# Feed-forward opening and block change written out tile by tile, x1's root mean square made in the attention stage, first group by token part

## The chip, the cores and the metric

The kernel runs on one core of one Trainium2 chip. The metric is the device time of one execution in microseconds, given as the median of three runs. A core has a matrix engine (PE, with its weight loads shown as PEld), a vector engine (DVE), a scalar engine (ACT), a general engine (POOL), and a sync engine (SP), whose queue issues most of the transfers. Each engine works through its own instructions in order and waits on semaphores that others raise.

## The reference, cut to what matters

One step of a streaming encoder layer: 2048 prompt frames (16 tiles of 128 rows) and 32 sample frames (tile 16, 32 rows), model width 1024. A token-mixing stage gives `x1 = x + rmsnorm(mix)`. Then comes the channel stage, with a hidden width of 4096:

```
u = rmsnorm(x1, norm_ffn_pre) @ w_up          # (tokens, 1024) @ (1024, 4096)
f = square(relu(u)) @ w_down                  # (tokens, 4096) @ (4096, 1024)
y = x1 + rmsnorm(f, norm_ffn_post)
rms_normalize(x) = x * rsqrt(mean(x * x) + eps)
```

## The kernel before, in words

Four stages follow one another, with a barrier between them: retention, projection of the attention inputs, `mix_phase` (attention, output projection, residual, x1 written to DRAM as `x1_scratch`) and `ffn_phase`. Only the last two are touched.

`mix_phase` works through 64 items (t, h): query tile t of 16, head h of 4. For each tile ACT squares and sums y (L1237, L1239), POOL raises the mean to the power -1/2 (L1154), DVE scales y (L1346), POOL adds the residual into `mix_xr` (L1161), and SP stores it (L1116), reloads `mix_xr` for the next tile (L1112) and then loads keys, queries and values of later tiles (L1095, L1098, L1101).

`ffn_phase` keeps all weights' use in 3-pass split form: each operand is a high part and a low part, and a product is three matmuls. Tokens are worked in two blocks: block 0 is tiles 0 to 7, block 1 is tiles 8 to 16. The hidden width is worked in 16 groups of 256 columns. In each block:

- The opening: for each tile x1 is loaded (L1629), ACT squares and sums it (L96, L99), POOL makes 1/rms (L108), DVE multiplies by it and the gain in place (L113), PE transposes it in 8 pieces into two PSUM banks (L120), ACT copies these out as the high part `ffn_hTh` (L130), and DVE subtracts to get the low part `ffn_hTl` (L136). Odd and even tiles use different pairs of the four banks `U`.
- For each group: `up` (PE, L1907) makes units of 24 matmuls into a bank of `U`. A unit is one half of the group's 256 columns for one part of the tokens (512 wide in block 0, 352 in block 1), so there are 4 units in block 0 and 6 in block 1. ACT takes the relu (L1744), DVE squares (L1823), ACT copies the high part (L1748), DVE subtracts for the low part (L1829). `down` (PE, L1923) makes two sums of 6 matmuls for each tile, and DVE adds them to the running sum `ffn_facc` (L1844; L1842 is the copy of the first group). The order on PE is up(g+1), then down(g).
- Weights of a group have one buffer: ACT copies the high part out of `ffn_raw` (L1717 up, L1723 down) and DVE makes the low part (L1793, L1800), once PE has read the last group's.

At the block change the last `down` of block 0 is interleaved with the opening of block 1, a tile of each in turn. ACT squares and sums the finished `ffn_facc` there (L1729, L1732), POOL makes 1/rms (L1681), and DVE normalises it in `hidden` of block 1's group 0 (L1806). POOL adds the residual (L1705), stores y (L1614) and loads the next residual tile (L1604). The `ffn_facc` of a tile is only written by block 1 once its store has landed.

## Time and profile before

| what | value |
|---|---|
| median of 3 runs | 3156.98 us (3156.43 to 3160.06) |
| the profiled execution's own time | 3157.81 us |
| its span | 3156.0 us |
| PE busy over the span | 92% |
| mix stage in the trace | about 930 to 1556.8 us |
| feed-forward stage in the trace | 1556.8 us to the end |

The profile gives for each instruction its start from the start of the span, its length, and in brackets the idle time of its engine just before it, with the instruction whose end released it. "issue" is a release that the profile doesn't show. The page has a row of PE's granted clock in tenths of full speed: 2.4 GHz is full, 1.2 GHz is half.

### The profile page before, as it was taken

The numbers are of one execution on the slowest core, as the hardware profiler recorded it, in microseconds if no ns is written. First come the engines' busy times: TensorE is split into PE (matmuls) and PEld (weight loads), VectorE is DVE, ScalarE is ACT, GpSimd is POOL, SyncE is SP. The second block draws the span as 40 slices with busy tenths as digits, with TensorE's granted clock in tenths as the row PEclk, the third lists the DMA queues.
The fourth block names the chain that finished last, engine by engine and source line by source line (L and its number), as shares of the span: only waits on it lengthen the run. The fifth ranks groups of instructions, "written<-read, shape, count | busy, mean of one in ns | idle before, by whom it ended". The sixth has DMA issues, their size and how long they took to land.

```text
span 3156.0 us, 39293 instructions
## 1 busy us (share of the span) xinstructions
PE 2898.0 (92%) x14977; PEld 2398.6 (76%) x14977; DVE 1515.4 (48%) x2983; ACT 926.9 (29%) x1838; POOL 318.4 (10%) x437
## 2 busy tenths in 40 slices
PE   5999995999968999999589999999968999999997
PEld 4888884778856766766468888888857998998995
DVE  3232333323246777777344444444456445445446
ACT  3222222222125555555331211211142211211212
POOL 0111110111112111111100000000013000000003
PEclk8999997999979999999789999999988999999999
DMA  4111003333332111110221111111124111111112
GB/s 147 32 34 34 34 21 116 111 113 123 117 122 75 64 64 47 52 41 21 107 68 46 54 40 53 40 53 53 40 69 136 51 40 41 53 40 40 53 54 97
DMA packets 105661, 204.64 MB, mean 65 GB/s; under 512 B 11024, under 2 KB 47888, under 8 KB 105552
## 3 DMA queue, kind: packets, MB, share of 16 engines
q1 hardware_dynamic: 103248, 194.79, 18.7%
q0 software_dynamic: 2304, 8.39, 0.8%
q8 instruction: 69, 1.13, 0.1%
q14 instruction: 40, 0.33, 0.0%
HBM read 168.28 MB, written 34.87 MB: 64 GB/s over the span
## 4 chain that ended last, share of the span: by engine, by line
PE 46%; DVE 2%; ACT 1%; DMA 1%; POOL 0%; issue 0%; SPq 0%; POOLq 0%
PE bank L1907 23%; PE bank L1923 22%; DVE ffn_facc L1806 1%; PE bank L120 1%; DVE ffnp_x L113 0%; ACT ffn_hTh L130 0%; DMA ffnp_x<-x_scratch 0%; DVE ffn_facc L1844 0%; POOL ffnp_rstd L108 0%; ACT ffn_relu L96 0%; ACT ffn_relu L1729 0%; DVE ffn_hidl L1829 0%; DMA ffn_raw<-in_w_up_dram 0%; DVE ffn_dnl L1800 0%; DVE ffn_upl L1793 0%
## 5 line engine op out<-in xcount | busy, mean ns | idle before, releaser
L1907 PE MATMUL bank<-ffn_hTh,ffn_uph 128*128 128x352 f32 (+1 forms) x1280 | 452.5, 354 | 23.3 <-DVE ffn_upl L1793 14.2
L1844 DVE TENSOR_TENSOR ffn_facc<-bank,ffn_facc 128x512 f32<-128x512 f32 x510 | 345.1, 689 | 233.4 <-PE bank L1923 233.0
L1907 PE MATMUL bank<-ffn_hTl,ffn_uph 128*128 128x352 f32 (+1 forms) x1280 | 451.5, 353 | 0.0
L1907 PE MATMUL bank<-ffn_hTh,ffn_upl 128*128 128x352 f32 (+1 forms) x1280 | 450.9, 352 | 0.0
L1923 PE MATMUL bank<-ffn_dnh,ffn_hidh 128*128 128x512 f32 x1088 | 427.3, 393 | 6.4 <-DVE ffn_dnl L1800 3.5
L1923 PE MATMUL bank<-ffn_dnh,ffn_hidl 128*128 128x512 f32 x1088 | 425.6, 391 | 0.0
L1923 PE MATMUL bank<-ffn_dnl,ffn_hidh 128*128 128x512 f32 x1088 | 425.5, 391 | 0.0
L1823 DVE SCALAR_TENSOR_TENSOR ffn_relu<-bank,ffn_relu 128x352 f32<-128x352 f32 (+1 forms) x160 | 94.5, 591 | 499.6 <-ACT ffn_relu L1744 499.6
L1907 PEld LDWEIGHTS bank<-ffn_hTh,ffn_uph 128*128 128x128 f32 x1280 | 242.6, 190 | 48.4 <-DVE ffn_upl L1793 14.5
L1907 PEld LDWEIGHTS bank<-ffn_hTl,ffn_uph 128*128 128x128 f32 x1280 | 242.7, 190 | 23.4
L1907 PEld LDWEIGHTS bank<-ffn_hTh,ffn_upl 128*128 128x128 f32 x1280 | 242.7, 190 | 22.7
L1744 ACT ACTIVATE ffn_relu<-bank 128x352 f32<-128x352 f32 (+1 forms) x160 | 83.0, 519 | 554.8 <-PE bank L1907 544.5
L1923 PEld LDWEIGHTS bank<-ffn_dnh,ffn_hidh 128*128 128x128 f32 x1088 | 205.8, 189 | 50.8 <-DVE ffn_facc L1844 4.6
L1723 ACT ACTIVATE ffn_dnh<-ffn_raw 128x1024 fp32r<-128x1024 f32 x64 | 64.5, 1052 | 607.8 <-PE bank L1923 590.5
L186 PE MATMUL bank<-retw_whi,retp_hTh 128*128 128x512 f32 x544 | 217.2, 399 | 26.1 <-DVE ret_rope_b L396 16.4
L1923 PEld LDWEIGHTS bank<-ffn_dnh,ffn_hidl 128*128 128x128 f32 x1088 | 205.4, 189 | 43.5
L1923 PEld LDWEIGHTS bank<-ffn_dnl,ffn_hidh 128*128 128x128 f32 x1088 | 205.5, 189 | 42.4
L1286 DVE TENSOR_SCALAR_CACHE_REDUCE mix_S<-bank 128x512 f32<-128x512 f32 (+4 forms) x320 | 175.3, 582 | 99.1 <-PE bank L1410 62.0
L186 PE MATMUL bank<-retw_wlo,retp_hTh 128*128 128x512 f32 x544 | 213.8, 393 | 0.0
L186 PE MATMUL bank<-retw_whi,retp_hTl 128*128 128x512 f32 x544 | 213.7, 393 | 0.0
L186 PE MATMUL bank<-dpw_whi,dpp_hTh 128*128 128x512 f32 x408 | 164.6, 403 | 8.9 <-DVE dpw_wlo L176 8.9
L1200 ACT ACTIVATE mix_S<-mix_S,mix_nm 128x128 f32<-128x128 f32 (+15 forms) x128 | 153.6, 1200 | 36.7 <-DVE mix_nm L1300 36.5
(196 smaller groups left out, 4462.3 us busy)
## 6 DMA issues: line engine op xcount, KB each, us to landing
ffn_raw<-in_w_up_dram SPq DMA_DIRECT2D x64, 512.0 KB, 4.4
ffn_raw<-in_w_down_dram SPq DMA_DIRECT2D x64, 512.0 KB, 4.1
ffnp_x<-x_scratch SPq DMA_DIRECT2D x24, 512.0 KB, 4.4
retp_x<-in_x_prompt_dram SPq DMA_DIRECT2D x16, 512.0 KB, 3.6
retw_raw<-in_w_in_dram SPq DMA_DIRECT2D x8, 1024.0 KB, 5.2
dpp_x<-in_x_prompt_dram SPq DMA_DIRECT2D x16, 512.0 KB, 5.1
dp_kst<-in_cache_diff_k_dram SPq DMA_DIRECT2D x32, 256.0 KB, 2.9
mix_xr<-in_x_prompt_dram SPq DMA_DIRECT2D x16, 512.0 KB, 3.3
```

Of the source, the lines that this page charges most:

```text
L120: last = self.nc.tensor.transpose(self.banks[2 * pair + k // 4][:, (k % 4) * P:(k % 4 + 1) * P], self.xn[u][:, k * P:(k + 1) * P], ident)
L186: last = self.nc.tensor.matmul(out, l[:, k, :], r[:, c, k, :], start=(k == 0 and q == 0), stop=(k == kt - 1 and q == 2))
L1200: nc.scalar.activation(S[n % 2][m][:, 0:width(t)], S[n % 2][m][:, 0:width(t)], ACT.Exp, bias=nm[n % 2][:, m:m + 1], accum_out=l[n % 2][:, ...
L1286: last = nc.vector.tensor_scalar(dst[:, c:c + whole], src[:, 0:whole], 1.0, None, ALU.mult, ALU.max, accum_out=mx[b][:, m, i + 1:i + 2])
L1723: nc.scalar.activation(dnh[:, i, :], raw[i][:], ACT.Copy).then_inc(s_whi, 1)
L1744: nc.scalar.activation(rh[i % 2][:, 0:w], U[i % s.ru][:, 0:w], ACT.Relu).then_inc(s_r, 1)
L1806: nc.vector.scalar_tensor_tensor(out=facc[:, i, :], in0=facc[:, i, :], scalar=rf[:, t:t + 1], in1=gain_b[:], op0=ALU.mult, op1=ALU.mult).t ...
L1823: nc.vector.scalar_tensor_tensor(out=rh[i % 2][:, 0:w], in0=U[i % s.ru][:, 0:w], scalar=0.0, in1=rh[i % 2][:, 0:w], op0=ALU.max, op1=ALU.m ...
L1844: nc.vector.tensor_tensor(out=part, in0=Dn[i % s.rd][:], in1=part, op=ALU.add).then_inc(s_add, 1)
L1907: last = nc.tensor.matmul(U[i % s.ru][:, 0:w], l[:, k, f * P:(f + 1) * P], r[:, k, c:c + w], start=(k == 0 and q == 0), stop=(k == 7 and q ...
L1923: last = nc.tensor.matmul(Dn[i % s.rd][:], l[:, f, tile * P:(tile + 1) * P], r[:, f, n * N:(n + 1) * N], start=(f == 0 and q == 0), stop=( ...
```

## The change

It has five parts.

1. x1's mean square is made in `mix_phase`: ACT `meansq_x` at head 3 of each tile and POOL `rstd_x`, kept in a column of `keep.rstd_x` for each tile. SP's reload of `mix_xr` now waits for the square as well.
2. `ffn_phase` has no mean square, so the chain for a tile is load, DVE `norm_x`, PE `x_transpose`, ACT `x_hi`, DVE `x_lo`. All tiles use one pair of banks, `U[2:4]`, and each half tile has its own wait.
3. The first group takes its units by token part (`first_units`), in banks `U[0]` and `U[1]`. The order on PE, ACT and DVE is written out by hand: in block 0 the first unit starts after tile 3.
4. Tiles 8 to 11 are loaded during block 0, and normalised by DVE in its last but one step. The block change is written out by hand as well, and the last two tiles of the last `down` come after the first group's units.
5. ACT's `meansq_f` and DVE's `norm_f` of block 0's result move from the opening and group 0 of block 1 to group 1, and the residual loads on POOL's queue wait for tiles 10 and 11 to be transposed.

```diff
@@ mix_phase, SP and ACT
                 def residual_rows(j):
+                    if j:
+                        sp.wait_ge(s_sx, j)
                     sp.dma_start(xr[0:rows(j), :], xv[j - 1] if j else x_s[0]).then_inc(s_x, 16)
...
+                def meansq_x(j):
+                    m = rows(j)
+                    act.wait_ge(s_x1, j + 1)
+                    nc.scalar.activation(junk[0:m, :], xr[0:m, :], ACT.Square, accum_out=sx[0:m, :]).then_inc(s_sx, 1)
+                    act.wait_ge(s_sx, j + 1)
+                    if j:
+                        act.wait_ge(s_rx, j)
+                    nc.scalar.activation(mean_x[0:m, :], sx[0:m, :], ACT.Copy, scale=1.0 / 1024,
+                                         bias=NORM_EPS).then_inc(s_mx, 1)
...
                     if h == 3:
+                        if t:
+                            meansq_x(t - 1)
                         y_out(t, 0)
@@ ffn_phase
         U, Dn = banks[0:4], banks[4:8]
+        TT = U[2:4]
...
+                self.first_units = [(f, c, w) for c, w in self.subs for f in range(FG)]
...
-            if t >= 2:
-                if b and i - 2 >= by_dve:
-                    eng.wait_ge(s_yd, i - 1 - by_dve)
-                else:
-                    eng.wait_ge(s_y, t - 1 if i >= 2 else blocks[b][0])
+            if b == 0 and i < 2:
+                eng.wait_ge(s_xT, 2 * (10 + i) + 2)
+            elif b and i - 2 >= by_dve:
+                eng.wait_ge(s_yd, i - 1 - by_dve)
+            else:
+                eng.wait_ge(s_y, t - 1 if i >= 2 else b1[0])
@@ ffn_phase, DVE
-                                for n in range(2 * i - 2, min(2 * i, ended.nb)):
+                                for n in range(max(2 * i - 4, 0), min(2 * i - 2, ended.nb)):
                                     norm_f(ended, n)
...
                         if not last:
-                            hidden(s, g + 1, 1 - e)
+                            hidden(s, g + 1, 1 - e, shapes[0] if s.b and isinstance(g, int) and g == 0 else None)
...
                                 accumulate(s, g, tile)
+                                if s.b == 0 and near and 1 <= tile <= 4:
+                                    norm_x(7 + tile)
@@ ffn_phase, PE
+                def x_transpose(t):
+                    pe.wait_ge(s_xn, t + 1)
+                    for b in range(2):
+                        if t:
+                            pe.wait_ge(s_lo, 2 * t - 1 + b)
+                        for k in range(4):
+                            last = nc.tensor.transpose(TT[b][:, k * P:k * P + rows(t)],
+                                                       x[slots[t]][0:rows(t), (4 * b + k) * P:(4 * b + k + 1) * P],
+                                                       ident[0:rows(t), 0:rows(t)])
+                        last.then_inc(s_xT, 1)
...
+                    if s.b == 0:
+                        for t in range(4):
+                            x_transpose(t)
+                        first_up(s, 0, range(0, 4))
+                        x_transpose(4)
+                        first_up(s, 0, range(4, 8))
+                        x_transpose(5)
+                        first_up(s, 1, range(0, 4))
+                        x_transpose(6)
+                        first_up(s, 1, range(4, 8))
+                        x_transpose(7)
+                        first_up(s, 2)
+                        first_up(s, 3)
+                        pe.wait_ge(s_pad, 4)
+                    else:
                         pe.wait_ge(s_h, s.u0)
...
+                        x_transpose(8)
+                        down(shapes[0], G - 1, 1, 0)
+                        x_transpose(9)
+                        down(shapes[0], G - 1, 1, 1)
+                        x_transpose(10)
+                        down(shapes[0], G - 1, 1, 2)
+                        first_up(s, 0, range(0, 4))
+                        x_transpose(11)
+                        first_up(s, 0, range(4, 8))
+                        x_transpose(12)
+                        first_up(s, 1)
+                        x_transpose(13)
+                        down(shapes[0], G - 1, 1, 3)
+                        first_up(s, 2)
+                        x_transpose(14)
+                        first_up(s, 3)
+                        x_transpose(15)
+                        down(shapes[0], G - 1, 1, 4)
+                        x_transpose(16)
+                        down(shapes[0], G - 1, 1, 5)
+                        first_up(s, 4)
+                        first_up(s, 5)
+                        down(shapes[0], G - 1, 1, 6)
+                        down(shapes[0], G - 1, 1, 7)
```

On PE at block 0's opening the order before is all eight tiles' transposes (here the last two tiles) and then the first unit:

```order
L120 MATMUL bank0<-kept_ident,ffnp_x2 128x128 x4
L120 MATMUL bank1<-kept_ident,ffnp_x2 128x128 x4
L120 MATMUL bank2<-kept_ident,ffnp_x3 128x128 x4
L120 MATMUL bank3<-kept_ident,ffnp_x3 128x128 x4
L1907 MATMUL bank0<-ffn_hTh,ffn_uph 128x512
```

In the changed kernel the same place on PE reads as follows, from tile 2 (`ffn_x2`) on:

```order
L2043 MATMUL bank2<-kept_ident,ffn_x2 128x128 x4
L2043 MATMUL bank3<-kept_ident,ffn_x2 128x128 x4
L2043 MATMUL bank2<-kept_ident,ffn_x3 128x128 x4
L2043 MATMUL bank3<-kept_ident,ffn_x3 128x128 x4
L2052 MATMUL bank0<-ffn_hTh,ffn_uph 128x512
```

The first unit moved from behind tile 7 to behind tile 3, and all transposes are in banks 2 and 3.

On DVE at the block change the order before is the up weights' low parts, then for each tile the norm, the two sums and the two low parts:

```order
L1793 TENSOR_TENSOR ffn_upl<-ffn_raw1,ffn_uph 128x1024
L113 SCALAR_TENSOR_TENSOR ffnp_x0<-ffnp_x0,ffnp_rstd0,ffnp_gain 128x1024
L113 SCALAR_TENSOR_TENSOR ffnp_x1<-ffnp_x1,ffnp_rstd1,ffnp_gain 128x1024
L1844 TENSOR_TENSOR ffn_facc<-bank4,ffn_facc 128x512
L1844 TENSOR_TENSOR ffn_facc<-bank5,ffn_facc 128x512
```

In the changed kernel, on DVE:

```order
L1865 TENSOR_TENSOR ffn_upl<-ffn_raw1,ffn_uph 128x1024
L1884 TENSOR_TENSOR ffn_hTl<-bank2,ffn_hTh 128x4x128
L1884 TENSOR_TENSOR ffn_hTl<-bank3,ffn_hTh 128x4x128
L1933 TENSOR_TENSOR ffn_facc<-bank4,ffn_facc 128x512
L1933 TENSOR_TENSOR ffn_facc<-bank5,ffn_facc 128x512
L1884 TENSOR_TENSOR ffn_hTl<-bank2,ffn_hTh 128x4x128
L1884 TENSOR_TENSOR ffn_hTl<-bank3,ffn_hTh 128x4x128
```

The norms have gone from the front of the block change, and the low parts of tile 8 stand straight behind the weights' low parts.

On DVE in group 1 of block 1 (352 wide; `ffn_gain_f` is the gain after the feed-forward) the changed kernel has the norms of block 0's result:

```order
L1911 TENSOR_TENSOR ffn_hidl1<-ffn_relu1,ffn_hidh1 128x352
L1891 SCALAR_TENSOR_TENSOR ffn_facc<-ffn_facc,ffn_rstd_f,ffn_gain_f 128x1024 x2
L1905 SCALAR_TENSOR_TENSOR ffn_relu1<-bank0,ffn_relu1 128x352
L1911 TENSOR_TENSOR ffn_hidl1<-ffn_relu0,ffn_hidh1 128x352
L1891 SCALAR_TENSOR_TENSOR ffn_facc<-ffn_facc,ffn_rstd_f,ffn_gain_f 128x1024 x2
```

Before, the same norms stood in group 0, on DVE:

```order
L1829 TENSOR_TENSOR ffn_hidl0<-ffn_relu0,ffn_hidh0 128x352
L1806 SCALAR_TENSOR_TENSOR ffn_facc<-ffn_facc,ffn_rstd_f,ffn_gain2 128x1024 x2
L1823 SCALAR_TENSOR_TENSOR ffn_relu0<-bank2,ffn_relu0 128x352
L1829 TENSOR_TENSOR ffn_hidl0<-ffn_relu1,ffn_hidh0 128x352
L1806 SCALAR_TENSOR_TENSOR ffn_facc<-ffn_facc,ffn_rstd_f,ffn_gain2 128x1024 x2
```

They moved one group later, with the same two norms behind a unit.

## Rows read from the trace of the kernel before

**Rows 1.** The page's busy times over the whole span.

```profile
PE 2898.0 (92%) x14977; PEld 2398.6 (76%) x14977; DVE 1515.4 (48%) x2983; ACT 926.9 (29%) x1838; POOL 318.4 (10%) x437
```

**Rows 2.** Waits of PE from 1550 us to the end: total, times, longest.

```profile
PE bank L120 <- DVE ffnp_x L113: 57.5, 15, 19.5
PE bank L1907 <- DVE ffn_upl L1793: 14.2, 1, 14.2
```

**Rows 3.** Chain of waits, 1540 to 2450 us: start, length, what.

```profile
1594.04 24.24 PE bank L1907 x96
1618.28 5.46 issue
...
2391.15 25.68 PE bank L1907 x144
2416.83 24.51 PE bank L1923 x108
```

**Rows 4.** Timeline of the opening of block 0.

```profile
1561.29 0.22 DVE L1852 MEMSET ffn_hidh<- 128x192 f32 x1 [10.76 <-DMA ffnp_gain<-in_norm_ffn_pre_dram]
...
1577.64 1.94 PE L120 MATMUL bank<-kept_ident,ffnp_x 128*128 128x128 f32 x8 [3.25 <-DVE ffnp_x L113]
1578.61 1.28 DVE L113 SCALAR_TENSOR_TENSOR ffnp_x<-ffnp_x,ffnp_rstd,ffnp_gain 128x1024 f32<-128x1024 f32 x1
1579.62 1.09 ACT L130 ACTIVATE ffn_hTh<-bank 128x512 fp32r<-128x512 f32 x2 [2.84 <-PE bank L120]
...
1592.69 1.29 DVE L136 TENSOR_TENSOR ffn_hTl<-bank,ffn_hTh 128x512 fp32r<-128x512 f32 x2 [1.15 <-ACT ffn_hTh L130]
```

**Rows 5.** Timeline of the block change, PE, DVE, ACT.

```profile
2286.87 0.39 PE L1923 MATMUL bank<-ffn_dnh,ffn_hidl 128*128 128x512 f32 x1
2288.38 2.36 DVE L1800 TENSOR_TENSOR ffn_dnl<-ffn_raw,ffn_dnh 128x1024 fp32r<-128x1024 f32 x2 [0.40 <-ACT ffn_dnh L1723]
2295.70 1.06 ACT L1717 ACTIVATE ffn_uph<-ffn_raw 128x1024 fp32r<-128x1024 f32 x1 [1.00 <-DMA ffn_raw<-in_w_up_dram]
2296.78 1.23 DVE L1793 TENSOR_TENSOR ffn_upl<-ffn_raw,ffn_uph 128x1024 fp32r<-128x1024 f32 x1 [0.83 <-ACT ffn_uph L1717]
2300.13 1.94 PE L120 MATMUL bank<-kept_ident,ffnp_x 128*128 128x128 f32 x8 [12.88 <-DVE ffnp_x L113]
...
2311.88 1.06 PE L120 MATMUL bank<-kept_ident,ffnp_x 128*128 128x128 f32 x8 [2.31 <-DVE ffnp_x L113]
```

**Rows 6.** Timeline of ACT: two units 352 wide at full clock.

```profile
2365.54 0.47 ACT L1744 ACTIVATE ffn_relu<-bank 128x352 f32<-128x352 f32 x1 [2.99 <-PE bank L1907]
2369.38 0.47 ACT L1744 ACTIVATE ffn_relu<-bank 128x352 f32<-128x352 f32 x1 [2.99 <-PE bank L1907]
```

**Rows 7.** Timeline of DVE and POOL, group 0 of block 1.

```profile
2363.07 2.48 DVE L1806 SCALAR_TENSOR_TENSOR ffn_facc<-ffn_facc,ffn_rstd_f,ffn_gain 128x1024 f32<-128x1024 f32 x2
2368.11 4.66 DVE L1806 SCALAR_TENSOR_TENSOR ffn_facc<-ffn_facc,ffn_rstd_f,ffn_gain 128x1024 f32<-128x1024 f32 x2
2369.26 2.42 POOL L1705 TENSOR_TENSOR ffn_facc<-ffn_facc,ffnp_x 128x1024 f32<-128x1024 f32 x1
2373.68 3.42 POOL L1705 TENSOR_TENSOR ffn_facc<-ffn_facc,ffnp_x 128x1024 f32<-128x1024 f32 x1 [0.59 <-DMA ffnp_x<-x_scratch]
2378.10 0.51 DVE L1823 SCALAR_TENSOR_TENSOR ffn_relu<-bank,ffn_relu 128x352 f32<-128x352 f32 x1
2378.54 2.72 DVE L1829 TENSOR_TENSOR ffn_hidl<-ffn_relu,ffn_hidh 128x352 fp32r<-128x352 f32 x1
```

**Rows 8.** Timeline of ACT and SP in the mix stage, tiles 2 and 9.

```profile
991.73 0.60 ACT L1232 ACTIVATE mix_y<-bank 128x512 f32<-128x512 f32 x1 [1.12 <-PE bank L1438]
...
993.98 0.60 ACT L1211 ACTIVATE mix_AT<-bank 128x512 f32<-128x512 f32 x1 [0.95 <-PE bank L1451]
...
1246.28 1.06 ACT L1237 ACTIVATE mix_junk<-mix_y 128x1024 bf16<-128x1024 f32 x1
...
1221.39 0.33 SPq L1112 DMA_DIRECT2D mix_xr<-in_x_prompt_dram  x1
1237.63 0.33 SPq L1098 DMA_DIRECT2D mix_qn<-q_scratch  x1
```

More of the change, by code:

```diff
@@ L1155, in rstd_y, with rstd_x @@
                                             op=ALU.pow).then_inc(s_ry, 1)
+                def rstd_x(j):
+                    m, t = rows(j), j - 1 if j else nt
+                    pool.wait_ge(s_mx, j + 1)
+                    nc.gpsimd.tensor_tensor(out=keep.rstd_x[0:m, t:t + 1], in0=mean_x[0:m, :], in1=half[0:m, :],
+                                            op=ALU.pow).then_inc(s_rx, 1)
                 def residual(j):
@@ L1733, in meansq_f, with relu @@
                                          bias=NORM_EPS).then_inc(s_mf, 1)
-                def hidden(s, g, e):
+                def relu(s, g, i, units):
+                    f, c, w = units[i]
                     k0 = s.u0 + g * s.ku
+                    bank = U[i % 2] if units is s.first_units else U[i % s.ru]
+                    act.wait_ge(s_u, k0 + i + 1)
+                    if i >= 2:
+                        act.wait_ge(s_hl, k0 + i - 1)
+                    nc.scalar.activation(rh[i % 2][:, 0:w], bank[:, 0:w], ACT.Relu).then_inc(s_r, 1)
@@ L1751, in _ @@
+                            if ended is not None:
+                                for n in range(2 * i - 2, min(2 * i, ended.nb)):
+                                    meansq_f(ended, n)
                 for s in shapes:
                     w0 = 2 * G * s.b
-                    if s.b:
-                        act.wait_ge(s_u, s.u0)
-                        act.wait_ge(s_hl, s.u0)
-                        up_hi(w0 + 1, s)
-                    pre.act_meansq(act, slot(s.t0), loads(s.t0), s.t0 + 1)
@@ L1758, in _ @@
-                    for i, t in enumerate(s.tiles):
-                        if i + 1 < s.nb:
-                            pre.act_meansq(act, slot(t + 1), loads(t + 1), t + 2)
-                        pre.act_hi(act, t, t + 1, rows(t), i % 2)
-                        if s.b == 0 and i == 1:
-                            up_hi(1, s)
-                        if s.b and i:
-                            meansq_f(shapes[0], i - 1)
-                    hidden(s, 0, 0)
+                    fu = s.first_units
@@ new lines, in up_unit, with first_up @@
+                def up_unit(bank, unit, ks):
+                    f, c, w = unit
+                    for k in ks:
+                        for q, (l, r) in enumerate(parts(uph, upl, hTh, hTl)):
+                            last = nc.tensor.matmul(bank[:, 0:w], l[:, k, f * P:(f + 1) * P], r[:, k, c:c + w],
+                                                    start=(k == 0 and q == 0), stop=(k == 7 and q == 2))
+                    return last
+                def first_up(s, i, ks=range(8)):
+                    f, c, w = s.first_units[i]
+                    if i == 0 and ks[0] == 0:
+                        pe.wait_ge(s_wlo, 4 * G * s.b + 2)
+                    if f == 0 and ks[0] == 0:
+                        pe.wait_ge(s_lo, 2 * (s.t0 + (c + w - 1) // P) + 2)
+                    if i >= 2 and ks[0] == 0:
+                        pe.wait_ge(s_h, s.u0 + i - 1)
+                    last = up_unit(U[i % 2], s.first_units[i], ks)
+                    if ks[-1] == 7:
+                        last.then_inc(s_u, 1)
@@ L1898, in up @@
                 def up(s, g):
-                    first = isinstance(g, int) and g == 0
-                    pe.wait_ge(s_wlo, 4 * G * s.b + (2 if first else 4 * g))
+                    second = isinstance(g, int) and g == 1
+                    pe.wait_ge(s_wlo, 4 * G * s.b + 4 * g)
                     k0 = s.u0 + g * s.ku
-                    for i, (f, c, w) in enumerate(s.units):
-                        if not (first and s.b == 0 and i < s.ru):
-                            pe.wait_ge(s_h, k0 + i + 1 - s.ru)
-                        for k in range(8):
-                            for q, (l, r) in enumerate(parts(uph, upl, hTh, hTl)):
-                                last = nc.tensor.matmul(U[i % s.ru][:, 0:w], l[:, k, f * P:(f + 1) * P],
-                                                        r[:, k, c:c + w], start=(k == 0 and q == 0),
-                                                        stop=(k == 7 and q == 2))
-                        last.then_inc(s_u, 1)
+                    for i, unit in enumerate(s.units):
+                        pe.wait_ge(s_h, k0 if second and i < s.ru else k0 + i + 1 - s.ru)
+                        up_unit(U[i % s.ru], unit, range(8)).then_inc(s_u, 1)
```

352 lines of the change are left out of this document (231 added, 121 removed).

## The prediction

> **What bounds the kernel now.** The page's busy times come first: PE is busy 92% of the span, DVE 48% [rows 1], so time is won only where PE stands idle. The waits of PE behind 1550 us say where that is in the feed-forward stage: 57.5 us in 15 waits of the transposes for x1's norm and 14.2 us in one wait for the up weights' low part [rows 2]. The chain of waits dates them. The first unit starts at 1594.04, group 0's four units end at 1618.28, and 5.46 us follow until up(1) [rows 3]. At the block change PE ends block 0's last but one `down` at 2287.26 (2286.87 + 0.39) and stands 12.88 us before the first transpose [rows 5]; each further tile waits about 2.3 us for its norm, as in the row at 2311.88 [rows 5]; up(1) of block 1 only starts at 2391.15 [rows 3]. The 14.2 us lie just ahead of that. The sum is made against the profiled execution's own time, 3157.81 us, of which 3156.0 is span; it is 0.83 us above the median 3156.98.
>
> **Opening of block 0.** The mean square and the 1/rms leave the tile's chain. DVE then waits for the gain's transfer, which landed at about 1561.3 when it was first in the queue [rows 4]. It is now second, behind x tile 0; with about 0.4 us for one more issue, the first norm starts at 1561.7. Ahead of the first unit DVE has five norms of 1.25 (1.28 with its start [rows 4]), four pairs of low parts of 1.25 (1.29 for two [rows 4]) and two weights' low parts, which I price at 2.3 (2.36 for two of that size [rows 5]): 5.0 + 6.25 + 2.3 = 13.6. About 0.65 is lost until the first tile is transposed and copied and 0.3 at tile 3, so the first unit starts at 1561.7 + 13.6 + 0.95 = 1576.3, 17.8 us earlier. From there the four units took 24.24 us [rows 3], their slow start included. Into them come four tiles' transposes. At full clock the eight cost 1.06, at half clock 1.94 [rows 4, 5]; I take 1.1, as PE is in steady work by then: 4.4 us. Unit 2 needs tile 7's low parts, queued on DVE behind `square` and norms: 1.5 us. The group ends at 1576.3 + 24.2 + 4.4 + 1.5 = 1606.4, which is 11.9 us earlier. The 5.46 us behind it stay, since the up weights' low part still needs the end of the last unit and no `down` lies there. **Gain 12.** Bounds: 6, if the transposes run at half clock (+3.5) and each tile waits half a microsecond more for its banks; 15, if the loads and transposes hide entirely.
>
> **Block change.** Tiles 8 to 11 are normalised by then. Their norms (1.28 each) stand on DVE in a `down` of block 0 whose sums leave it idle half the time, so they cost nothing there. If that cover failed they would cost 4 x 1.28 = 5. From 2287.26 the first transpose goes at once. `down` then waits for its weights until 2290.74 [rows 5]: 2.4 us. After tile 0's two sums (2.7) PE waits for tile 8's low parts, since these stand on DVE behind the up weights' low parts, which end at 2298.0 [rows 5]; with 0.65 for the first low part tile 9's transpose starts at 2298.7: 5.2 us idle. That is the first wait left, and what is late is the weight's transfer. After it I find none over 1 us: PE always has a half unit or a `down` while ACT and DVE finish the tile. PE's own work to up(1) is 8 full transposes of 1.06, one of a quarter's width (8.7 in all), 16 sums of 1.36 (24.51 / 18 [rows 3]) = 21.8, and six units of 3.84 (from relu to relu [rows 6]) = 23.0: 53.5. With 2.4 + 5.2 idle, 0.8 for tile 16's norm and 3 us for half clock after the two pauses, 64.9: up(1) starts at T = 2352.2. The up weights' low part for it is ready by about T - 1, made during the last four sums, so the 14.2 us vanish. This is 39 us ahead of 2391.15.
>
> **What group 1 gives back.** up(1) takes 23.0 instead of 25.68 [rows 3] (+2.7), so it ends 41.6 us earlier. Then `down` needs DVE, which now has the eight norms of the finished result behind the units. With the first at T + 13 (unit 1's end, two squared sums on ACT, relu of unit 2), DVE has 8 x 1.25 for norms, and 8 x 0.44 for squares and low parts: 13.5, to T + 26.5. But POOL's residual adds run at the same time. A pair of norms takes 2.48 us alone and 4.66 with an add of 2.42 in it; a low part, both of whose inputs are in SBUF, takes 2.72 where others take some 0.5; a square, with an input in a PSUM bank, keeps its 0.51 [rows 7]. So an add takes about 2.1 from DVE, and six fall in: 12.6, and DVE reaches the first sum at T + 39. PE ends up(1) at T + 23 and has three banks to fill, to T + 27: 12 us idle. Behind the first two sums stand the next up weights' low parts (2.3, and an add's 2.3); three banks cover some of it, and I take 2 more. **Net of the block change and group 1:** 41.6 - 14 = 27.6, say 27. Bounds: 41 if the adds cost nothing, 18 if all eight cost 2.42 and the pauses keep PE at half clock twice as long.
>
> The Trainium skill, page "SBUF — State Buffer", section "Who interferes with whom", says that a VectorE instruction with two SBUF inputs and a GpSimd one that reads SBUF exclude each other for a whole instruction. By it eight adds of 2.42 would be 19.4 us if none fell into DVE's own idle time, and the sums out of PSUM would stay free. The rows agree: the low part waits, the square doesn't.
>
> **Mix stage.** ACT gains per tile a square as at L1237 (1.06) and a read of the sum and a scale (0.2 each), about 1.4, 17 times: 24. It stands just ahead of `y_out` of head 3. At tile 2 ACT stands 1.12 us before that instruction and 0.95 before the copy after the next exp [rows 8], 2.07 together, and this is the least of the 15 tiles from 1 on. So it costs 0; without that cover it would cost 24. POOL's 17 powers of 0.55 lie in its waits. SP reloads `mix_xr` at 1221.39 and then stands until 1237.63 for PE [rows 8]; the reload moves by some 4 us and nothing behind it moves. At the stage's end the last mean square runs beside the store of x1 and its landing: I take 0, at most 0.5.
>
> **Sum.** 3157.8 - 12 - 27 = 3118.8; against the median 3118.
>
> **Rivals.**
> - *The adds are cheap.* If POOL's adds fall into DVE's own waits, `down` starts at once: 12 more, 3106. For it: ACT paces group 1 too (two squared sums, a relu and a copy per unit of 3.84), so DVE has idle time. Against it: 4.66 against 2.48.
> - *One pair of banks.* Before, tiles alternate between two pairs; now a tile's transposes wait for the last one's low parts. If a tile is then serial (1.94 + 1.09 + 1.29 = 4.3 [rows 4] against DVE's 2.5), the four tiles ahead of the first unit cost 7 more and the later ones 4, and in group 1 the stores of y are late as well: 3126 to 3132. Against it: each half has its own wait, so PE fills one bank while the other is emptied. The Trainium skill, page "Perfetto Trace Analysis", section "Matmuls", advises rotating independent groups through different banks so that the emptying overlaps; this change gives up half of the rotation, and by that rule its opening would be worth 5 and not 12.
> - *Nothing won.* The deferred norms, adds and stores take back all: `down` of group 0 waits for stores of y that land later than T + 60. It takes adds 7 us apart and a wait of 39. Against it: two adds are 4.4 apart (2369.26 and 2373.68 [rows 7]), and `down` of group 0 reaches the last tile only at about T + 59.
> - *Slower: the mix stage's reload on the path.* SP's reload of `mix_xr` waits for ACT's square, 4.2 us later, and the key and query loads stand behind it. If each of 16 tiles became 4.2 us longer, that is 67 against a gain of 39: 3186. It decides from 2.4 us per tile. Against it: SP stands 16 us behind the reload for PE anyway [rows 8].
>
> **How the numbers follow.** Chances: forecast 0.62 (3110 to 3126), adds cheap 0.12, banks or stores dearer 0.20, nothing won 0.03, slower 0.03. A difference of 0.2% (6 us) is about what can be told from none. Faster therefore 0.94, same 0.03, slower 0.03. The range goes from the cheap adds, 3104, to 3132 (dearer banks).
>
> **What would show it.** The first unit should start near 1576 and up(1) of block 0 near 1612; the block change should show waits of 2.4 and 5 us and up(1) near 2340 (2352 less the opening's 12); `down` of group 0 in block 1 should wait some 12 us for DVE, with norms of 4.7 a pair beside adds. In the mix stage ACT should be busier by 24 us with the end at 1557. It is wrong if that stage ends later than 1560, if the first unit waits for loads, or if `down` doesn't wait.

## The result

The changed kernel took 3139.36 us (median of 4 runs, 3133.6 to 3139.44), beside 3158.52 for the kernel before on the same chip: a ratio of 0.9928 over all runs, 95% interval 0.9914 to 0.9941 (the two medians alone give 0.9939). The forecast was 3118, with a range up to 3132, so the time lies 7 us outside the range. The sign was right; of the gain of 39 us that was forecast, 19 came. The profiled execution took 3139.41 us, with a span of 3137.6. All reading below is made against it.

### The profile after

The busy times of the whole span, as in [rows 1]:

```profile
PE 2911.7 (93%) x14977; PEld 2397.1 (76%) x14977; DVE 1516.0 (48%) x2983; ACT 925.8 (30%) x1838; POOL 315.0 (10%) x437
```

The span is 18.4 us shorter, and yet PE is busy 13.7 us *more*, with the same 14977 matmuls. Waits went away and matmuls became longer. That is the first sign of something that the forecast had no term for.

The waits of PE from 1550 us on, which answer to [rows 2] (total, times, longest):

```profile
PE bank L2043 <- DVE ffn_x L1878: 17.9, 2, 17.5
PE bank L2088 <- DVE ffn_facc L1931: 15.2, 1, 15.2
PE bank L2043 <- DVE ffn_hTl L1884: 7.2, 4, 2.9
PE bank L2088 <- DVE ffn_dnl L1872: 6.2, 2, 3.5
PE bank L2052 <- DVE ffn_upl L1865: 5.5, 1, 5.5
PE bank L2052 <- DVE ffn_hTl L1884: 3.2, 2, 1.7
```

Of the 57.5 us 17.9 are left, nearly all of them the one wait at the stage's start, and the 14.2 us at the block change are gone; the 5.5 us in the fifth line are the 5.46 us of "issue" that [rows 3] has behind group 0 of block 0. The new line is the second: in group 1 of block 1 `down` stood 15.2 us until VectorE came to its sums.

The chain of waits, pieces that answer to [rows 3, 5] (start, length, what):

```profile
1558.93 5.39 DMA ffn_gain_x<-in_norm_ffn_pre_dram
...
1579.26 5.46 PE bank L2052 x12
...
1615.54 14.57 PE bank L2052 x54
1639.86 22.25 PE bank L2088 x96
1662.11 22.26 PE bank L2052 x96
...
2289.07 5.36 DMA ffn_raw<-in_w_up_dram
...
2297.52 1.16 PE bank L2043 x8
2298.68 4.36 PE bank L2088 x12
...
2349.26 11.49 PE bank L2052 x72
2391.52 23.97 PE bank L2088 x90
2415.49 22.91 PE bank L2052 x144
...
2726.04 25.02 PE bank L2088 x108
```

Two groups of block 0 in the kernel before, from the same view, for the comparison:

```profile
1648.42 21.81 PE bank L1923 x96
1670.23 22.26 PE bank L1907 x96
```

A `down` of 96 matmuls takes 22.25 us where it took 21.81; one of 108 takes 25.02 where it took 24.51 [rows 3]. The `up` beside it kept its 22.26. TensorE's granted clock is full in both. The difference is small, but block 0 has 16 groups and block 1 as many.

The span is made up of stretches whose ends both chains date. With them the gap of 20.6 us (forecast 3118.8 for the profiled execution, measured 3139.4) can be laid out. Positive is time lost against the forecast:

| stretch | forecast | measured | gap |
|---|---|---|---|
| end of the attention stage | 1556.9, unchanged | 1558.6 | +1.7 |
| opening, to `up`(1) of block 0 | 12 won | 9.9 won | +2.1 |
| groups 1 to 15 of block 0 | nothing | 15 downs of +0.44 | +6.6 |
| block change, to `up`(1) of block 1 | 39 won | 40.2 won | -1.2 |
| group 1 of block 1, to `up`(2) | 12 given back | 16 given back | +4 |
| the rest of block 1 | nothing | 14 downs of +0.51, and the end | +7.4 |

These add up to the 20.6. "12 given back" is the block change's 39 less the net 27 of the forecast; the 16 are 66.2 us from 2349.26 to 2415.49, less the 50.2 from 2391.15 to 2441.34 in the kernel before. Of the 4 us of that row 0.5 is again the longer `down`; most of the rest is TensorE's wait, 15.2 us where 12 was forecast.

### The profile page after: what moved, and what is told of

Its sections match the earlier page's. It is cut to its first block, busy times and chain, and to the rows that moved or that the text cites. A ratio compares the mean times of both kernels' runs of the same rounds, so it can differ in the third digit from the quotient of the medians.

```text
span 3137.6 us, 39331 instructions
## 1 busy us (share of the span) xinstructions
PE 2911.7 (93%) x14977; PEld 2397.1 (76%) x14977; DVE 1516.0 (48%) x2983; ACT 925.8 (30%) x1838; POOL 315.0 (10%) x437
## 4 chain that ended last, share of the span: by engine, by line
PE 47%; DVE 2%; POOL 1%; DMA 0%; ACT 0%; issue 0%; SPq 0%; POOLq 0%; DVEq 0%
PE bank L2088 24%; PE bank L2052 23%; DVE ffn_facc L1891 1%; PE bank L2043 0%; POOL ffn_facc L1738 0%; DVE ffn_facc L1933 0%; DVE ffn_upl L1865 0%; DVE ffn_hTl L1884 0%; DMA ffn_gain_x<-in_norm_ffn_pre_dram 0%; DMA ffn_raw<-in_w_up_dram 0%; DVE ffn_dnl L1872 0%; POOL ffn_rstd_f L1720 0%; DVE ffn_x L1878 0%; DMA ffn_x<-x_scratch 0%; DVE ffn_facc L1898 0%
## 5 line engine op out<-in xcount | busy, mean ns | idle before, releaser
L2088 PE MATMUL bank<-ffn_dnh,ffn_hidh 128*128 128x512 f32 x1088 | 431.8, 397 | 24.2 <-DVE ffn_facc L1931 15.2
L2088 PE MATMUL bank<-ffn_dnh,ffn_hidl 128*128 128x512 f32 x1088 | 432.6, 398 | 0.0
```

The costliest lines, as they stand in the source:

```text
L2088: last = nc.tensor.matmul(Dn[i % s.rd][:], l[:, c:c + P], r[:, f, n * N:(n + 1) * N], start=(f == 0 and q == 0), stop=(f == FG - 1 and q = ...
```

## Experiments

### Why `down` became longer

The new code changed two things that `down` reads. The hidden buffers are flat, with rows of 1056 columns instead of 1152 and in another order, and all large buffers begin 32 bytes above a multiple of 64, where they began at one.

**Address.** The changed kernel with 32 bytes put in:

```diff
+        sb("shift", [P, 8])
         hTh, hTl = sb("hTh", [P, 8, tokens], F32R), sb("hTl", [P, 8, tokens], F32R)
```

> The changed kernel with 32 unused bytes per partition ahead of the transposed activations, so that every large buffer of the feed-forward stage begins at a multiple of 64 bytes, as in the kernel before, instead of 32 above one; nothing else differs. Theory 1 (the addresses make the down matmuls dear): a down of 108 matmuls takes 24.51 us again instead of 25.02, one of 96 takes 21.81 instead of 22.25, so about 14 us come back and the time is near 3125. Rival (the flat layout of the hidden buffers does it): both stay at 25.02 and 22.25, and the time stays at 3139.

Measured: 3140.55 us, ratio 0.995 (0.9934 to 0.9967); the downs stay at 22.25 and 25.02. The mirror image is the kernel before with the same line.

> The kernel before with 32 unused bytes per partition ahead of the transposed activations, so that its large buffers lie 32 bytes above multiples of 64. By the theory of addresses its downs grow from 24.51 to 25.02 us and from 21.81 to 22.25, and the time by 14 us to about 3172; by the theory of the layout nothing changes, 3158.

Measured: 3163.03 us, ratio 1.0014 (1.0004 to 1.0023), which is some 4 us where the theory of addresses wanted 14. Its downs stay at 21.81 and 24.51, and the span of its profiled execution is 3155.3, 0.7 less than before. By these rows the theory of addresses fell; what made its other executions longer (up to 3167.1 us) no trace shows.

**Layout.** The old buffers in the new kernel:

```diff
-        hidden_flat = [[sb(f"hid{n}{u}", [P, FG * tokens + P - dec], F32R) for n in "hl"] for u in range(2)]
+        hid3 = [[sb(f"hid{n}{u}", [P, FG, nb_max * P], F32R) for u in range(2)] for n in "hl"]
```

> The changed kernel with the hidden activations in the four buffers of the kernel before (2 x 1152 columns each, high parts of both generations first, then low parts), all still 32 bytes above a multiple of 64; the square's scratch output lies in the gain's buffer, to make room. If the layout makes the down matmuls dear, their rows go back to 24.51 and 21.81 us and the time to about 3125; if it is the addresses modulo 64, the rows stay at 25.02 and 22.25 and the time at 3139.

Measured: 3127.35 us, ratio 0.9907 (0.9891 to 0.9924). Its chain of waits:

```profile
1643.73 21.81 PE bank L2088 x96
...
2719.30 24.51 PE bank L2088 x108
```

The layout it is: the median is 12 us under that of the changed kernel and 13 under that of a_shift32, which ran on the same chip. In the traces the feed-forward stage alone is 16.0 us shorter (3126.6 less its start at 1563.57, against 3137.6 less 1558.56). Of these, 14 are the downs of groups 1 to 15, as in the table above; the others lie in the opening, the block change and group 1. Two more runs part its two halves, the order of the four buffers and the pitch of their rows.

> The changed kernel with its flat hidden buffers (rows of 1056 columns) allotted in the order of the kernel before: high 0, high 1, low 0, low 1. If the distance between the high and the low part (8832 bytes in the changed kernel, 18432 before, 17664 here) makes the down matmuls dear, a down of 108 goes back to 24.51 us and one of 96 to 21.81. If the 1056-column rows do it, they stay at 25.02 and 22.25.

> The changed kernel with hidden rows of 1152 columns, as before, but in the changed kernel's order: high 0, low 0, high 1, low 1 (9216 bytes from high to low); the square's scratch output lies in the gain's buffer. If the row pitch is what counts, down takes 24.51 and 21.81 us; if the order is, 25.02 and 22.25.

Measured: the order alone, 3142.6 us in one run, with downs of 22.26 and 25.04; the pitch alone, 3128.0 us, with 21.81 and 24.51. It is the pitch. Which pitches are good was then tried with one for each parity of the group:

```diff
+        pitch = (1088, 1184)
+        hidden_flat = [[sb(f"hid{n}{u}", [P, max(2 * pitch[u], pitch[u] + nb_max * P)], F32R) for n in "hl"] for u in range(2)]
...
-                            c = f * tokens + tile * P
+                            c = f * pitch[e] + tile * P
```

> The changed kernel with hidden rows of 1088 columns in the buffers of even groups and 1184 in those of odd ones (4352 and 4736 bytes; 1056 is 4224, 1152 is 4608). If any pitch above 1056 will do, both kinds of down take 24.51 us. If the pitch must be a whole number of 512 byte rows, so that all 128-column slices keep their offset within 512 bytes, both stay at 25.02. If a multiple of 256 bytes is enough, the even ones take 24.51 and the odd ones 25.02.

Measured: 3135.65 us. The chain of waits, groups 0 and 1 of block 0 and two neighbours of block 1:

```profile
1643.56 21.81 PE bank L2090 x96
...
1687.63 22.25 PE bank L2090 x96
...
2724.44 25.04 PE bank L2090 x108
...
2772.39 24.51 PE bank L2090 x108
```

Neighbouring groups differ by just the 0.44 and 0.5 us. A larger pitch isn't better as such: 1088 columns (4352 bytes) are good and 1184 (4736) are not. Of the four pitches, 1088 and 1152 are multiples of 256 bytes, 1056 and 1184 are not. With 1184 every slice of the second hidden row begins 128 bytes off those of the first, modulo 256. Yet it isn't only the second row's matmuls that are long: in the odd groups of block 0 the six matmuls of a sum come 231.2 ns apart on average in the first row and 232.3 in the second, where the even groups have 227.4 and 227.0.

**The other operand.** `up` had 231.9 ns for each 512-column matmul in both kernels. Its moving operand is `hTh`/`hTl`, and that has rows of 1056 columns too.

> The changed kernel with rows of 1152 columns in the transposed activations instead of 1056; the hidden rows stay at 1056. To make room, the output norm multiplies by the first gain, and the second isn't loaded. The up matmuls 512 wide take 231.9 ns each before and after the change, the slow figure of down. If the pitch of the moving operand does that, an up of 96 takes 21.81 us instead of 22.26 in block 0; if only the stationary operand's pitch counts, up stays at 22.26. Down stays at 22.25 and 25.02 in either case.

Measured: 3136.84 us. The chain of waits in block 0:

```profile
1642.93 22.25 PE bank L2085 x96
1665.18 21.77 PE bank L2049 x96
```

(This kernel makes room by using one gain for both norms.) Now `up` is the shorter one, 21.77 us, and `down` keeps its 22.25. The old kernel had paid this all along in block 0.

### What group 1 gave back

The DVE and POOL timelines of the changed kernel in group 1 (T, the start of `up`(1), is 2349.26):

```profile
2362.14 2.47 DVE L1891 SCALAR_TENSOR_TENSOR ffn_facc<-ffn_facc,ffn_rstd_f,ffn_gain_f 128x1024 f32<-128x1024 f32 x2
...
2368.32 0.57 POOL L1720 TENSOR_TENSOR ffn_rstd_f<-ffn_meansq_f,ffn_half 128x1 f32<-128x1 f32 x1
2368.86 2.40 POOL L1738 TENSOR_TENSOR ffn_facc<-ffn_facc,ffn_x 128x1024 f32<-128x1024 f32 x1
2368.93 3.42 DVE L1891 SCALAR_TENSOR_TENSOR ffn_facc<-ffn_facc,ffn_rstd_f,ffn_gain_f 128x1024 f32<-128x1024 f32 x1 [0.48 <-POOL ffn_rstd_f L1720]
2371.55 0.60 POOL L1650 DMA_DIRECT2D out_dram<-ffn_facc  x1 [0.30 <-POOL ffn_facc L1738]
2372.15 0.54 POOL L1640 DMA_DIRECT2D ffn_x<-x_scratch  x1
...
2390.79 1.27 DVE L1931 COPY ffn_facc<-bank 128x512 f32<-128x512 f32 x2
```

Two norms alone take 2.47 us; five single ones take 3.36 to 3.42 each. Each of the five begins when POOL's 1/rms ends, and just then POOL begins its next add. POOL makes the 1/rms of tile t + 2 between the load behind add t - 1 and add t, so norm and add start together every time. VectorE reaches the first sum (line L1931) at T + 41.5; the forecast said T + 39.

**All 1/rms ahead of the adds.**

```diff
-                    for t in s.tiles[:2]:
+                    lead = s.tiles if s.b == 0 else s.tiles[:2]
+                    for t in lead:
                         rstd_f(t)
                     for i, t in enumerate(s.tiles):
-                        if i + 2 < s.nb:
+                        if s.b and i + 2 < s.nb:
                             rstd_f(t + 2)
```

> The changed kernel with all eight powers of block 0's output norm ahead of GpSimd's first residual add, instead of each two tiles ahead. If group 1 loses its 15.2 us because each norm waits for a power that stands behind an add in GpSimd's queue, the norms end with ScalarE's last mean square (T + 23) plus one or two adds' contention, VectorE ends hidden(1) about 9 us earlier, at T + 32, TensorE's wait falls from 15.2 to 6 us, and the time to about 3130. If it is the adds' contention itself, wherever the powers stand, the norms stay near 3.4 us each and the wait stays over 12 us, the time at 3137 to 3139.

Measured: 3134.1 us, ratio 0.9927 (0.9911 to 0.9944). DVE's timeline:

```profile
2384.23 1.27 DVE L1932 COPY ffn_facc<-bank 128x512 f32<-128x512 f32 x2
...
2397.42 1.29 DVE L1932 COPY ffn_facc<-bank 128x512 f32<-128x512 f32 x2 [4.62 <-DMA out_dram<-ffn_facc]
```

VectorE came to the sums at T + 31, as the first theory said, but TensorE's waits only fell from 15.2 to 10.2 us, in six pieces. Behind them is something that neither theory had: a sum of block 1 overwrites the rows of `facc` that a store of block 0 still reads. The adds now began so late that their stores were the next in line. So the adds must start early, and the 1/rms must not stand behind them.

**Four, two, two.** On the kernel with the old hidden buffers:

```diff
+                    ahead = iter(s.tiles)
                     for i, t in enumerate(s.tiles):
-                        if i + 2 < s.nb:
-                            rstd_f(t + 2)
+                        for _ in range((3 if i == 0 else 1) if s.b else (4, 2, 2)[i] if i < 3 else 0):
+                            n = next(ahead, None)
+                            if n is not None:
+                                rstd_f(n)
```

> The kernel of run b_hid_3d (3127) with GpSimd's powers of block 0 in the order four, add 0, two, add 1, two, add 2, and the rest of the adds. With all eight ahead VectorE reached the first sum 6 us earlier, at T + 35, but the adds and stores ended so late that the sums of down(0) stood for stores. Worked out here: norms 0 to 3 lie ahead of the adds, 4 to 7 beside adds 1 and 2, VectorE reaches the first sum at T + 34 and the last store lands at T + 49, about when tile 7's sum comes. TensorE then loses some 8 us in place of 15.2, and the time is 3120 to 3121. Rival: stores bound it, as with all powers ahead, and the waits sum up to over 12 us: 3125 to 3127.

Measured: 3119.6 us, ratio 0.9866 (0.9849 to 0.9882), 8 us under run b_hid_3d. In the traces 6.6 of them lie in group 1: `up`(1) to `up`(2) took 65.7 us there and takes 59.0 here. TensorE's wait is one of 8.9 us, and VectorE reaches the sums at T + 35.

**Without the adds.** What the rest is made of:

```diff
-                        nc.gpsimd.tensor_tensor(out=facc[0:rows(t), i, :], in0=facc[0:rows(t), i, :],
-                                                in1=xe[i % 2][0:rows(t), :], op=ALU.add).then_inc(s_y, 1)
+                        if s.b:
+                            nc.gpsimd.tensor_tensor(out=facc[0:rows(t), i, :], in0=facc[0:rows(t), i, :],
+                                                    in1=xe[i % 2][0:rows(t), :], op=ALU.add).then_inc(s_y, 1)
+                        else:
+                            pool.sem_inc(s_y, 1)
```

> The kernel of run f_powers_4_2_2 without GpSimd's eight residual adds of block 0 (that block's output is then without its residual); stores and loads stay. If the adds take from VectorE what stays of group 1's wait (8.9 us), each pair of norms takes 2.5 us, VectorE reaches the first sum at T + 28 and TensorE waits under 3 us, so the time is 3113 to 3115. If the eight norms and the 2 x 6 squares and low parts are simply too much for the group, the wait stays over 6 us.

Measured: 3110.68 us in one run, some of it an early end of the attention stage. The 8.9 us shrink to three waits:

```profile
PE bank L2092 <- DVE ffn_facc L1935: 1.6, 3, 0.9
```

All four pairs of norms take 2.47 or 2.48 us, and VectorE reaches the sums at T + 27.2. So 7.3 of the 8.9 us were the adds, and VectorE's own load hides behind TensorE's `up`(1) and first banks but for 1.6 us. The Trainium skill, page "SBUF — State Buffer", section "Who interferes with whom", has a VectorE instruction with two SBUF inputs and a GpSimd one that reads SBUF exclude each other for a whole instruction; by that rule the pair of norms should drop to its time alone once no add runs, and the trace agrees.

### Why the attention stage ended later

It ended at 1556.86 us before and at 1558.56 after. In all but one of the other kernels with the changed attention stage it ended later still, mostly near 1562, with TensorE's waits in the stage as they were (47.8 us in 23 waits for `mix_S` before, 47.0 in 23 after). Windows of PE at the change from tile 8 to tile 9, first in the kernel before, then in the changed one (PE busy, count, granted clock as a share of full speed, DMA share, GB/s):

```profile
1216.00:1218.00 2.00, 1.24 (x6) 1.00 0.00 0
1218.00:1220.00 2.00, 0.38 (x4) 1.00 0.24 98
1220.00:1222.00 2.00, 1.97 (x13) 1.00 0.41 164
1222.00:1224.00 2.00, 2.00 (x12) 1.00 0.77 253
```

```profile
1216.00:1218.00 2.00, 1.01 (x6) 1.00 0.01 4
1218.00:1220.00 2.00, 0.59 (x4) 1.00 0.36 150
1220.00:1222.00 2.00, 1.97 (x8) 0.53 0.28 113
1222.00:1224.00 2.00, 2.00 (x7) 0.62 0.00 0
```

TensorE paused 2.4 us in both (4 us less 1.62 and less 1.60 busy). Before, it went on at full clock; after, about 3.4 us ran at the lower of its two levels. That costs (1 - 0.53) x 2 + (1 - 0.62) x 2 = 1.7 us, which is this tile's share. (The stage itself is 2.7 us longer in this trace, 634.1 us from its gain's load at 924.43 where it was 631.5 from 925.41; the stages ahead of it happened to end 1.0 us earlier.)

The changed attention stage alone, in front of the old feed-forward stage:

> The kernel before with the changed attention stage alone: x1's mean squares and powers are made there as in the changed kernel, but nothing reads them, and the feed-forward stage is the old one. If the 24 us of ScalarE work are covered, as predicted, the feed-forward stage starts at 1556 to 1557. If the work moves PE's pauses into stretches of half clock, it starts at 1559 to 1564 and the whole is 2 to 7 us longer than before, 3160 to 3165.

Measured: 3167.87 us, the feed-forward stage starting at 1562.93: 6 us later. The squares behind the output copy in ACT's order, on the kernel of run f_powers_4_2_2:

```diff
+                        y_out(t, 0)
                         if t:
                             meansq_x(t - 1)
-                        y_out(t, 0)
```

> The kernel of run f_powers_4_2_2 (3119.6) with x1's mean square of a tile behind the first output copy of the next in ScalarE's order instead of ahead of it. Its attention stage ended at 1563 like most with the mean squares. If the squares' place ahead of the output copy costs these 6 us, the stage ends at 1557 and the time is 3114. If it is only a matter of which pauses of TensorE the clock answers with a stretch at half speed, TensorE's waits stay the same 47 us and the end lies anywhere from 1557 to 1564.

Measured: 3124.76 us, start at 1564.78. The place isn't it. Another trace of the kernel before, unchanged:

> The kernel before, unchanged, for another trace of its attention stage. In two traces with the old stage the feed-forward stage starts at 1556.9 and 1556.1 us, in eleven with the mean squares at 1558.6 to 1564.8. If the mean squares cost the difference, it starts at 1556 to 1557 again; if the spread is the chip's, anywhere up to 1564.

Measured: 3157.08 us, start at 1556.62. And the squares and powers left out, on the fastest kernel (below):

```diff
+                nc.gpsimd.memset(keep.rstd_x[:], 1.0)
...
-                    if j:
-                        sp.wait_ge(s_sx, j)
...
-                        if t:
-                            meansq_x(t - 1)
```

> The kernel of run v_pitch_per_block without x1's mean squares and powers in the attention stage; the root mean square is taken as 1, so the feed-forward stage computes with x1 unnormalised in scale, and SyncE's reload waits for no square. Three traces of the old attention stage ended 5 us earlier than the mean of thirteen with the squares (1556.5 against 1561.9). If the squares cost that, the feed-forward stage starts at 1556 to 1557 and all ends 5 us earlier than with them. If it is the lottery of which pause the clock answers, it starts anywhere between 1556 and 1565.

Measured: 3107.86 us, start at 1557.13, and no drop of the clock at that tile change:

```profile
1220.00:1222.00 2.00, 1.97 (x13) 1.00 0.53 217
1222.00:1224.00 2.00, 2.00 (x11) 1.00 0.65 211
```

Four traces have no squares there (before, c_before_shift32, q_before_again, w_no_squares). They start the feed-forward stage at 1556.1 to 1557.1, mean 1556.7. Fourteen traces with the squares ahead of the output copy start it at 1558.1 to 1565.6, mean 1561.9. In these profiled executions the squares go with 5 us, though TensorE waits no longer for anything.

The times of the other executions don't bear this out as a cost in general. The traced executions of the kernel before took 3157.1 and 3157.8 us, but its 40 others on record average 3160.3 (3155.0 to 3166.1). The seven kernels with the squares that ran more than once go the other way: their 22 other executions average 2.0 us less than the traced ones. If the feed-forward stage takes as long in each execution as in its kernel's trace, the attention stage ends at about 1559.6 on average without the squares and 1559.8 with them. This is an estimate, since no trace dates the stage in those executions, but by it the traces of the kernel before were early ones, and a cost of the squares is not shown. The one run of k_mix_alone speaks for a cost (it lies above all seven runs of the kernel before on its chip, 3158.3 to 3164.0), and it can't decide.

Which of TensorE's pauses are followed by the lower clock also differs between kernels whose attention stage is the same code; why, these runs don't show.

### The opening

The first norm waited 5.39 us for the gain, which was second in SP's queue. The gain first, on the kernel of the next section:

```diff
+                        sp.dma_start(gain_x[:], gain_pre.to_broadcast([P, 1024])).then_inc(s_gain, 16)
                         x_tile(0)
-                        sp.dma_start(gain_x[:], gain_pre.to_broadcast([P, 1024])).then_inc(s_gain, 16)
```

> The kernel of run n_pitch_1088 with the gain's transfer ahead of tile 0's in SyncE's queue. The first norm waited for the gain, 5.4 us behind its issue. If the second transfer in the queue always lands last, the norm waits for tile 0 instead and starts as late, 5.8 us after the stage's start; if the gain itself is the slow one, it starts 0.4 us earlier. The time is that of n_pitch_1088 within 1 us apart from where the attention stage ends.

Measured: the first norm starts 5.76 us after the stage, against 5.74 with the gain second, and waits for tile 0's transfer, 5.29 us. Whichever is second lands last. (The run took 3122.79 us, with a start of the stage at 1565.58.)

### Faster kernels

First one pitch for all, 1088 columns:

```diff
+        pitch = -(-tokens // 64) * 64
...
-        hTh, hTl = sb("hTh", [P, 8, tokens], F32R), sb("hTl", [P, 8, tokens], F32R)
+        hTh, hTl = sb("hTh", [P, 8, pitch], F32R), sb("hTl", [P, 8, pitch], F32R)
...
+        hid_flat = [[sb(f"hid{n}{u}", [P, pitch + nb_max * P], F32R) for n in "hl"] for u in range(2)]
```

> The kernel of run f_powers_4_2_2 (3119.6) with rows of 1088 columns (4352 bytes, a multiple of 256) in both the transposed activations and the hidden buffers; the three small statistics share one buffer to make room. If a row pitch that is a multiple of 256 bytes makes each 512-column matmul 5 ns shorter whichever operand it feeds, up of 96 takes 21.8 us in block 0 instead of 22.26 and down stays at 21.81 and 24.51: 16 x 0.48 = 7.7 us, near 3112. Rival: the moving operand needs another multiple (1152 columns are 9 times 512 bytes), up stays at 22.26 and the time at 3119.

Measured: 3114.59 us, ratio 0.9853 (0.9836 to 0.987). The chain of waits:

```profile
1638.69 21.76 PE bank L2092 x96
1660.45 21.76 PE bank L2056 x96
...
2701.66 24.50 PE bank L2092 x108
2726.16 23.23 PE bank L2056 x144
```

Block 0's `up` fell to 21.76 us as expected. Block 1's, whose units are 352 wide, rose from 22.92 to 23.23, and 15 x 0.31 = 4.7 us of the 16 x 0.5 = 8 go back. So block 0 alone got another pitch, as a second view of the same buffers:

```diff
-        hTh, hTl = sb("hTh", [P, 8, tokens], F32R), sb("hTl", [P, 8, tokens], F32R)
+        hT = sb("hTh", [P, 8 * tokens], F32R), sb("hTl", [P, 8 * tokens], F32R)
+        views = [[a[:, 0:8 * n].rearrange("p (k n) -> p k n", k=8) for a in hT] for n in (len(b0) * P, tokens)]
```

> The kernel of run f_powers_4_2_2 (3119.6) with block 0's transposed activations in rows of 1024 columns (4096 bytes), a second view of the same buffers; block 1 keeps its 1056, since in run n_pitch_1088 rows of 1088 made its 352 wide up of 144 longer, 23.23 us instead of 22.92, while block 0's up of 96 fell to 21.76. If a multiple of 256 bytes is the rule for the 512 wide matmul, up takes 21.8 us in block 0 and 22.92 in block 1: 16 x 0.5 = 8 us less than 3119.6, near 3112. Rival: rows of exactly 4096 bytes are dear again for both operands and up stays at 22.26, 3119.

Measured: 3112.02 us, ratio 0.9841 (0.9828 to 0.9855), the lowest median with the full computation. The interval overlaps that of n_pitch_1088, but the traces tell them apart: from its start to the end of the span the feed-forward stage takes 1548.3 us here and 1553.7 there. Its chain:

```profile
1643.09 21.76 PE bank L2090 x96
1664.85 21.76 PE bank L2054 x96
...
2703.57 24.51 PE bank L2090 x108
2728.08 22.92 PE bank L2054 x144
```

## Why the prediction was right in sign and wrong in size

- **What bounds the kernel.** Right: the gain lay in TensorE's waits around the opening and the block change. 9.9 and 40.2 us came of them, 50 in all; what the total lacks was lost in other places.
- **Block change, 39 us.** Right: 40.2. The two waits foreseen at 2.4 and 5.2 us measured 2.67 and 2.93:

```profile
2289.10 0.80 PE L2088 MATMUL bank<-ffn_dnh,ffn_hidh 128*128 128x512 f32 x1 [2.67 <-DVE ffn_dnl L1872]
2297.52 1.16 PE L2043 MATMUL bank<-kept_ident,ffn_x 128*128 128x128 f32 x8 [2.93 <-DVE ffn_hTl L1884]
```

The second is shorter than foreseen because the 12 matmuls between the two ran at half clock and took 5.5 us (2289.10 to 2294.59) where 2.8 is usual; the 12 behind it took 4.36. Waits and half clock together are 9.9 us against the forecast's 10.6 (2.4 + 5.2 + 3). The cause named for them is right too: the weights' transfer (2289.07, 5.36 us) is in the chain.

- **Opening, 12 us.** Mis-sized: 9.9. The gain landed 5.39 us behind its issue and the first norm started 5.8 us after the stage's start, where 4.8 was counted; the units and transposes took 30.8 us instead of 30.1. The bound of 6 to 15 held it.
- **"Groups 1 to 15 cost the same".** This step was never written down, and it is the one that failed: the sum took each unchanged group at its old price. The new hidden buffers have rows of 1056 columns, and each `down` matmul takes 231.7 ns instead of 227. That is 15 x 0.44 = 6.6 us in block 0 and 14 x 0.51 = 7.1 in block 1, two thirds of the gap. Runs h_pitch_1152 and g_flat_order settle it. With the old pitch (run b_hid_3d) the kernel measured 3127.35 us, inside the forecast's range, so this one term put at nothing decides that the time missed it.
- **What group 1 gives back.** The mechanism was right: adds take VectorE's time from the norms, the wait is for `facc`, and without adds it is 1.6 us. The size was off: 15.2 for that wait against 12, and 16 given back against 12 (0.5 of it the longer `down`). The step "six adds fall in, 2.1 each" left out that the 1/rms stands behind an add in POOL's queue, which adds 0.5 to 1.0 us of waiting per norm and starts each of the last five norms together with an add.
- **Rival: adds cheap.** Refuted by the same rows. **Rival: nothing won**, by late stores: not here, but d_powers_first brought just that mechanism in, at 10.2 us.
- **Rival: one pair of banks.** The time went beyond its band, but not for its reason. The opening is worth 9.9 us, not 5, and the transposes' four waits for low parts are 7.2 us in all, the two longest of them (2.9 each) for one that VectorE makes behind the up weights' low parts. The Trainium skill, page "Perfetto Trace Analysis", section "Matmuls", advises rotating independent groups through different banks; the prediction made 5 us of the opening by that rule, and the trace's 9.9 doesn't bear out that price.
- **Mix stage at 0, at most 0.5.** Too low for this trace: the stage ends 1.7 us later, with one stretch at the lower clock that the kernel before doesn't have. The cover for ACT's work was real, since TensorE's waits didn't grow. "Covered" was taken to mean "free", and the traces with the squares end 5 us later on average; whether that holds for the untraced executions is open, as said above.

## What to carry to other kernels

When a change reshapes a buffer, take the row pitch of everything that TensorE reads as a part of the change: compare the mean time of *unchanged* matmuls first, because a loss of 2% there is larger than most waits. When a chain of small operations shares a queue with a long one, look at what each waits for *and* at what starts at the same moment; here an order of four, two, two was worth 8 us, and both extremes were worse. Work that hides under another engine's wait can go with other stretches of low clock on TensorE; but before one trace of each kernel is read as a cost of a few microseconds, the times of the untraced executions should show it too.

## What the runs showed of the hardware

- A 512-column fp32r matmul takes 227 ns or 231.8, depending on the row pitch of its operand. For the stationary one (hidden rows): 1088 and 1152 columns give 227, 1056 and 1184 give 231.8. For the moving one (activations): 1024, 1088 and 1152 columns give 227, 1056 gives 231.9. A multiple of 256 bytes fits all eight; other rules that fit them too aren't excluded. Where the buffer starts, at 0 or 32 modulo 64 bytes, changed nothing in either kernel.
- A 352-column matmul doesn't follow it: `up` of 144 takes 22.92 us at a pitch of 1056, 22.95 at 1152 and 23.23 at 1088. Why is open.
- A pause of 2.4 us of TensorE was followed by full clock in one kernel and by 3 to 4 us at half clock in another at the same place of the program, with the same work on both sides of it.
